# Attention of a hybrid encoder block: another deal of rows, tiles, banks and output turns

## The reference, cut to what matters

```python
h = rmsnorm(x, g_pre)
c_q, c_kv, k_pe, gate_a, hq, hf, hi, gate_b, merge_logits = split(h @ w_in)
...                                   # q, k (96 wide) and v (64 wide) for 8 heads
def one_block(args):                  # 128 queries of 2048, for each head
    sc = einsum('bhqd,bhkd->bhqk', qi, k) * scale
    sc = where(key_chunk <= query_chunk, sc, -inf)    # chunks of 64 frames
    p = softmax(sc)
    return einsum('bhqk,bhkd->bhqd', p, v)
y_a = (attn * silu(gate_a)) @ w_branch_a
...                                   # a second branch, a gated recurrence: y_b
y = (gate_0 * y_a + gate_1 * y_b) @ w_out
x = x + rmsnorm(y, g_post)
```

## Time and profile before

| | us |
|---|---|
| median of 3 runs | 2501.58 |
| lowest and highest | 2498.33, 2503.56 |
| profiled execution, its own time | 2496.99 |
| its span, first to last instruction | 2495.2 |

### The profile page before, as it was taken

One profiled execution on the slowest core, in us unless ns is written; L12 is line 12 of the kernel. 1 busy time (PEld: TensorE's weight loads), 2 busy tenths in 40 slices (PEclk: granted clock), 3 DMA queues, 4 the chain that ended last, 5 costly groups with the idle time before them and its releaser, 6 DMA issues. The chain is left out here.

```text
span 2495.2 us, 33539 instructions
## 1 busy us (share of the span) xinstructions
PE 2236.1 (90%) x11536; PEld 1853.5 (74%) x11536; DVE 1077.6 (43%) x1842; ACT 916.3 (37%) x1715; POOL 406.5 (16%) x254
## 2 busy tenths in 40 slices
PE   6999999999979999999678849988898875899998
PEld 5888888777868888888557737777777764677787
DVE  6000000000034554454356427767677766565663
ACT  7111111011034444444353216655655654343441
POOL 1222223214011111111022200000000003420220
PEclk9999999999989999999789859999999997899999
DMA  5222221223023333332665460223232107663751
GB/s 178 76 77 71 68 70 60 97 97 109 34 73 98 96 99 97 97 93 67 206 200 173 139 153 7 68 65 67 65 66 42 33 18 227 179 198 114 193 168 68
DMA packets 212448, 256.32 MB, mean 103 GB/s; under 512 B 38944, under 2 KB 137888, under 8 KB 208672
## 3 DMA queue, kind: packets, MB, share of 16 engines
q1 hardware_dynamic: 187616, 208.31, 29.4%
q10 hardware_dynamic: 23616, 43.00, 4.6%
q0 software_dynamic: 1152, 4.19, 0.5%
HBM read 157.41 MB, written 98.04 MB: 102 GB/s over the span
## 5 line engine op out<-in xcount | busy, mean ns | idle before, releaser
L1728 ACT ACTIVATE pT<-turn 128x512 fp32r<-128x512 f32 (+1 forms) x320 | 158.4, 533 | 203.5 <-PE turn L1855 202.9
L1785 DVE TENSOR_TENSOR pT<-turn,pT 128x512 fp32r<-128x512 f32 (+1 forms) x320 | 184.1, 606 | 92.5 <-ACT pT L1728 92.4
L66 PE MATMUL bankD<-hT_hi,shared_w_hi 128*128 128x512 f32 x512 | 212.2, 415 | 11.7 <-POOLq L676 11.7
L66 PE MATMUL bankA<-hT_hi,shared_w_hi 128*128 128x512 f32 x544 | 212.7, 391 | 0.0
L67 PE MATMUL bankA<-hT_lo,shared_w_hi 128*128 128x512 f32 x544 | 212.0, 390 | 0.0
L68 PE MATMUL bankA<-hT_hi,shared_w_lo 128*128 128x512 f32 x544 | 211.9, 390 | 0.0
L1771 DVE TENSOR_REDUCE chunk_min<-scores 128x1 f32<-128x512 f32 (+2 forms) x320 | 184.5, 606 | 61.3 <-PE scores L1841 37.3
L68 PE MATMUL bankD<-hT_hi,shared_w_lo 128*128 128x512 f32 x512 | 201.7, 394 | 0.0
L67 PE MATMUL bankD<-hT_lo,shared_w_hi 128*128 128x512 f32 x512 | 200.9, 392 | 0.0
L66 PE MATMUL scores<-k_sb,q_sb 96*128 96x512 f32 (+2 forms) x320 | 132.4, 414 | 73.3 <-ACT probs L1718 36.3
L1718 ACT ACTIVATE probs<-scores,least 128x1024 f32<-128x1024 f32 (+2 forms) x192 | 167.1, 871 | 38.5 <-DVE least L1778 37.4
(11 more groups left out here) (233 smaller groups left out, 4659.3 us busy)
## 6 DMA issues: line engine op xcount, KB each, us to landing
projT<-stage ACTq DMA_DIRECT2D x68, 256.0 KB, 2.4
shared_w_raw<-in_w_in_dram SPq DMA_DIRECT2D x32, 512.0 KB, 4.4
projT<-d_stage ACTq DMA_DIRECT2D x64, 256.0 KB, 2.4
e_l_in<-projT SPq DMA_DIRECT2D x64, 256.0 KB, 4.6
gateTok<-stage ACTq DMA_DIRECT2D x32, 256.0 KB, 2.0
shared_w_lo<-hgTok SPq DMA_DIRECT2D x16, 512.0 KB, 3.4
knT<-b_out SPq DMA_DIRECT2D x32, 256.0 KB, 2.8
vTok<-b_out SPq DMA_DIRECT2D x32, 256.0 KB, 2.9
```

Of the source, the lines that this page charges most:

```text
L66: pe.matmul(out, a_hi, b_hi, start=first, stop=False)
L1728: act.activation(pT[:, at % RING, 0, r0 * P:], turn[:, TURN_AT[tile] % 3, r0 * P:], ACT.Copy)\
L1785: dve.tensor_tensor(pT[:, at % RING, 1, r0 * P:], turn[:, TURN_AT[tile] % 3, r0 * P:], pT[:, at % RING, 0, r0 * P:].bitcast(F32), ALU.subt ...
```

## The change

The pieces of the diff stand in the order of the code: the schedule and the banks, the load of `fold`, then ACT's, DVE's and PE's parts.

```diff
-LED = 2 * TPB
+TURN_RING = 3
+LED = 2 * TPB + 1
...
+    TILES_AT = {9: 4, 10: 3, 11: 3, 12: 4, 13: 3, 14: 3, 15: 4,
+                0: 0, 1: 0, 2: 1, 3: 2, 4: 2, 5: 2, 6: 2, 7: 3, 8: 4}
...
     def s_bank(i, c):
-        return c + (r if b == 0 else 2 * (r % 2) if b == 1 else 0)
+        return (c + (r if b == 0 else 2 * (r % 2) if b == 1 else 3 * r if b == 2 else 0)) % 4
+    def chunks_of(i, piece):
+        b = i // TPB
+        cut = min(1 if s_bank(i, 0) == 3 else 2, b + 1)
+        return (0, cut) if piece == 0 else (cut, b + 1)
...
+        fold = sb("fold", [P, VD])
...
+                for half in range(2):
+                    sp.dma_start(fold[half * VD:(half + 1) * VD, :], ident_d[0:VD, 0:VD]).then_inc(const_in, 16)
...
-                        for tile in tiles[:AHEAD]:
-                            hi_part(h, tile)
                         if done is not None:
...
                             act.activation(oT[:], o_acc[:], ACT.Copy).then_inc(o_copied, 1)
+                        for tile in tiles[:AHEAD]:
+                            hi_part(h, tile)
...
-                            act.activation(o_lo[:], turn[:, at % 3].rearrange("p (t n) -> p t n", n=P)[:, :, VD:], ACT.Copy)\
-                               .then_inc(o_lo_ready, 1)
...
-                    dve.tensor_tensor(o_sum[:], turn[:, at % 3].rearrange("p (t n) -> p t n", n=P)[:, :, 0:VD], o_lo[:],
-                                      ALU.add).then_inc(o_sum_ready, 1)
...
-                    dve.tensor_tensor(o_out[:, b % 2], o_sum[:], inv[:].unsqueeze(2).to_broadcast([P, TPB, VD]), ALU.mult)\
-                       .then_inc(o_ready, 1)
+                    dve.tensor_tensor(o_out[:, b % 2], turn[:, at % TURN_RING, 0:TPB * VD].rearrange("p (t n) -> p t n", n=VD),
+                                      inv[:].unsqueeze(2).to_broadcast([P, TPB, VD]), ALU.mult).then_inc(o_ready, 1)
...
+                        if not tiles:
+                            for tile in before:
+                                values(h, tile, u)
+                            before = []
 ...
-                        for tile in tiles:
+                        for tile in before:
+                            if tile[0] == done:
+                                values(h, tile, u)
+                        for tile in tiles[:TURN_RING]:
                             transposes(h, tile)
                         for tile in before:
-                            values(h, tile, u)
+                            if tile[0] != done:
+                                values(h, tile, u)
+                        for tile in tiles[TURN_RING:]:
+                            transposes(h, tile)
...
-                                last = pe.transpose(turn[:, at % 3, r * P:(r + 1) * P], oT[:, r * P:(r + 1) * P], ident[:])
+                                last = pe.matmul(turn[:, at % TURN_RING, r * VD:(r + 1) * VD], oT[:, r * P:(r + 1) * P], fold[:], start=r == 0,
+                                                 stop=r == TPB - 1, skip_group_check=True)
```

More of the change, by code:

```diff
@@ L1529 @@
 AHEAD = 2
-LED = 2 * TPB
+TURN_RING = 3
+LED = 2 * TPB + 1
 def attention_schedule():
[L1537 to L1544, removed]
+    TILES_AT = {9: 4, 10: 3, 11: 3, 12: 4, 13: 3, 14: 3, 15: 4,
+                0: 0, 1: 0, 2: 1, 3: 2, 4: 2, 5: 2, 6: 2, 7: 3, 8: 4}
+    tiles = [(b, j) for b in range(NB) for j in range(TPB * (b + 1))]
+    steps = []
+    for row in [*range(LED, TT), *range(LED)]:
+        steps.append([row, tiles[:TILES_AT[row]], None, None])
+        tiles = tiles[TILES_AT[row]:]
     steps += [[None, [], None, None], [None, [], None, None]]
@@ L1587, in pieces_before @@
             if t < i:
-                b = t // TPB
-                used = {s_bank(t, x) for x in range(2 * piece, min(2 * piece + 2, b + 1))}
+                used = {s_bank(t, x) for x in range(*chunks_of(t, piece))}
                 if s_bank(i, c) in used:
@@ L1708, in exponentials @@
                     b, r = i // TPB, i % TPB
-                    first, end = 2 * piece, min(2 * piece + 2, b + 1)
+                    first, end = chunks_of(i, piece)
                     n = min(end * BLK, (i + 1) * P) - first * BLK
-                    bank = s_bank(i, 0)
-                    src = scores[:].rearrange("p b n -> p (b n)")[:, (bank + first) * BLK:(bank + first) * BLK + n]
+                    bank = s_bank(i, first)
+                    src = scores[:].rearrange("p b n -> p (b n)")[:, bank * BLK:bank * BLK + n]
                     if piece == 0:
@@ L1727, in hi_part @@
                     act.wait_ge(pv_done, h * TILES + (at + 2))
-                    act.activation(pT[:, at % RING, 0, r0 * P:], turn[:, TURN_AT[tile] % 3, r0 * P:], ACT.Copy)\
+                    act.activation(pT[:, at % RING, 0, r0 * P:], turn[:, TURN_AT[tile] % TURN_RING, r0 * P:], ACT.Copy)\
                        .then_inc(hi_ready, 1)
@@ L1735, in head @@
                     for i, tiles, done, o_block in STEPS:
-                        for tile in tiles[:AHEAD]:
-                            hi_part(h, tile)
+                        row_of = h + 1 if i is not None and i < LED else h
                         if done is not None:
@@ L1742, in head @@
                             act.activation(oT[:], o_acc[:], ACT.Copy).then_inc(o_copied, 1)
+                        for tile in tiles[:AHEAD]:
+                            hi_part(h, tile)
                         if i is not None and (more or i >= LED):
[L1744 removed]
+                            exponentials(row_of, i, 0)
                         for tile in tiles[AHEAD:]:
                             hi_part(h, tile)
[L1747 to L1753, removed]
[L1754 to L1755 removed]
+                        if i is not None and i >= 2 * TPB and (more or i >= LED):
+                            exponentials(row_of, i, 1)
                 for i in range(LED):
                     exponentials(0, i, 0)
+                    if i >= 2 * TPB:
+                        exponentials(0, i, 1)
                 with act.Fori(0, HEADS - 1) as h:
@@ L1784, in lo_part, with inverse @@
                     dve.wait_ge(hi_ready, h * TILES + (at + 1))
-                    dve.tensor_tensor(pT[:, at % RING, 1, r0 * P:], turn[:, TURN_AT[tile] % 3, r0 * P:],
+                    dve.tensor_tensor(pT[:, at % RING, 1, r0 * P:], turn[:, TURN_AT[tile] % TURN_RING, r0 * P:],
                                       pT[:, at % RING, 0, r0 * P:].bitcast(F32), ALU.subtract).then_inc(turn_read, 1)
-                def outputs(h, b):
-                    at = TURN_AT["o", b]
+                def inverse(h, b):
                     n = h * NB + (b + 1)
@@ L1811, in head @@
                 def head(h, more):
-                    for i, tiles, _, o_block in STEPS:
+                    for i, tiles, done, o_block in STEPS:
                         if i is not None and (more or i >= LED):
@@ L1854, in transposes @@
                     for r in range(max(0, j - TPB * b), TPB):
-                        last = pe.transpose(turn[:, at % 3, r * P:(r + 1) * P], probs[b][:, r, j * P:(j + 1) * P], ident[:])
+                        last = pe.transpose(turn[:, at % TURN_RING, r * P:(r + 1) * P], probs[b][:, r, j * P:(j + 1) * P], ident[:])
                     last.then_inc(turned, 1)
```

17 lines of the change are left out of this document (9 added, 8 removed).

## The result

| | before | after |
|---|---|---|
| median, us | 2499.95 (4 runs) | 2481.68 (4 runs) |
| profiled execution, us | 2496.99 | 2480.62 |
| its span, us | 2495.2 | 2478.8 |

The ratio is 0.9926, 95% interval 0.9904 to 0.9947: faster, by 0.7%. One of the four executions of after took 3248.95 us at a mean granted clock of 0.649 and is left out of the ratio; the median of the other three is 2480.62. The forecast was 2482.

The account below looks back on a forecast made before the run. TensorE sets the pace, through its waits, work and clock. A gain of 4 us net of waits and work plus 15 from the clock, 19 us, takes 2496.99 to 2478, median 2482; range 2465 to 2499.

Parts of the forecast that it names:

- seven heads at full clock: Seven heads of the attention: each goes from 68.2 to 67.4 us, 0.8 less, 5.6 for seven.
- last head: The final head, with no successor's rows 0 to 8: TensorE stands through copy and lo part, 1.4 us worse.
- Rotating banks and row 8 ahead: Row 9's step: its chunks go to banks 3, 0, 1, left long ago; row 8 fills TensorE before the last tiles.
- the 1.62 and the 0.29: TensorE's waits per head for bank 0, at row 9 (1.62 us) and row 10 (0.29); both were to go.
- The new waits: Waits inside a head that the change creates: 4.85 us, with refilling about 5.7.
- The fourth tile: Tile (0, 3) at row 9 wants the bank of (0, 0): a new wait of 1.0 us.
- the second pieces: Last chunks of rows 10, 13 and 14 wait 0.5, 0.5 and 0.1 us for the second pieces of rows' work.
- The early copy: ScalarE's copy ahead of hi parts: row 11 waits about 1.2 us, row 14 1.0; old 0.78, 1.78 and 0.74 go.
- The output product: Block ends: four products take 0.89 us, 0.45 more per block, 1.8 a head; removing copy and add gains nothing.
- Four passes: Skill's FP32 rule, not taken: at a record's length per pass, four output products take 1.8 us, 32 blocks 42 more.
- The clock: TensorE's clock in the heads: a quarter of the 19.8 us lost stays; gain 15, bounds 0 to 19.8.
- rival A: Waits move and the clock falls as often, transposes not counting as busy: only 4 us gained, 2497.6; chance 0.15.

Follow-up runs that it names:

- padding alone: The kernel before with four extra matmuls of 128 columns ahead of each block's output turn and no output product: 2525.05 us, ratio 1.0099.

## Why the prediction was right, and where its steps were off

The time was forecast within 2 us, whichever median is taken, and that is in good part luck: two errors of 7 and 8 us cancel. For the profiled execution, in us, said and measured: seven heads at full clock -5.6 and -12.6; clock -15, clock and loop end -6.9; last head +1.4 and +0.8; first wait +0.2 and +2.8; the first rows and the chance ahead of them, which no step had, -2.4 and +1.9. Together -19 and -16.4.

**Rotating banks and row 8 ahead.** Right that the 1.62 and the 0.29 go, the one by row 8's place, the other by the banks. Both edits are needed: with either undone 1.1 to 1.9 us a head come back.

**The new waits were over-sized.** The fourth tile waits 0.87 (said 1.0) and row 11 0.74 (said 1.2); row 14 waits 0.58 (said 1.0), the second pieces 0.14 or nothing (0.5, 0.5 and 0.1), and (2, 10) 0.12 (0.35). I had added ScalarE's durations end to end, with 0.2 us between engines. In its timeline the copy, two hi parts and the piece start 0.49 and then 0.96 us after one another, each a little ahead of the other's end: from the copy's start to the piece's end it is 2.58 us, not 2.8. That is half of the 0.4 at row 14; the rest isn't accounted for. The head came to 66.4, not 67.4, and the seven heads gained 12.6 instead of 5.6.

**The early copy.** It frees `o_acc` for block 2 (0.96 without it) and shortens row 11's wait, as costed; its price is the 0.58 at row 14.

**The output product.** 0.88 us for eight records, from 1924.46 to the next matmul at 1925.34, as taken from the earlier trace rows. Four passes, each as long as a record, would have been 1.8; that reading is not borne out, and how many passes a record holds the trace doesn't show. The step that failed is the one that costed the removed copy and add at nothing: in the new order they are worth 3.1 us a head (1.8 of work saved and still 1.3 lost), because VectorE stands for `o_lo` ahead of the minima and lo parts that come next in its list. That no wait of the earlier trace rows names them didn't make them free: with the product alone in the old order, row 15's wait of 0.74 shrank to 0.11, with padding alone to 0.36.

**The clock.** Right that falls behind row 9 and row 13 end. Wrong that a quarter of the loss stays: 23.8 us at 0.50 are left of 47.6, half. Of these, 10.2 stand at the loop end that stood still, and 13.6 behind a head's end, where I had called the waits too short. The trace of before already had such a fall, which the prediction overlooked when it said that no wait of 0.8 or less was followed by one. Its longest stretch at 0.50 begins behind the waits of 0.72 and 0.67 at a head's end, ahead of row 9's:

```profile
1774.06 0.49 PE L66 MATMUL scores<-k_sb,q_sb 96*128 96x512 f32 x1 [0.67 <-PE turn L1896]
...
1775.40:1785.60 10.20, 8.87 (x35) 7.79 (x34) 5.66 (x13) 3.95 (x10) 0.00 (x0) 0.50 0.93 186
```

Nor do such waits force a fall: with the old outputs in the new order they are there too (0.31 and 0.69), and five of seven heads keep 1.00. What decides is open. The loss itself was 21.6, not 19.8, as the earlier trace rows lack the first of the seven heads, which takes 70.1. The rule on transposes (rival A) would have left the falls behind row 11 and row 14, next to twelve transposes; there are none. But the waits there are 0.74 and 0.58, not the 1.0 to 1.2 that the rival counted on, so this doesn't refute the rule.

**The start and the last head.** With `fold` the first row waits about 2.5 us longer, not 0.2; its issue alone doesn't explain that, and what does is open. The last head lost 0.8 of the 1.4.

**What no step had** is the loop end, worth 6 us when it happens: the head with it takes 72.7, the other heads of that trace 66.4 to 69.4.

## What to carry to other kernels

When the clock of TensorE falls behind a wait, price that wait with the fall: filling 0.77 us of it with useless matmuls gave 8 us here by the medians, and placing a row's scores there 11 to 14, some of it perhaps luck at the loop ends. Weigh an intermediate by what stands behind it in each engine's list, not by whether the engine is busy on average. And count the instructions that an edit adds to a long loop body: 32 matmuls more cost a stop of 4 to 6 us at some loop ends.

## What the runs showed of the hardware

- TensorE's loop over two heads stands 3.8 to 5.8 us at some loop ends with 768 or 774 matmul records in its body, in eight of ten traces, with 9 more packets in the instruction queue for each. All 11 stops are at the ends of the first two passes of three, 20 places in these traces. With 736 or 746 records, in four traces, it never stood more than 0.71 at a loop end. The limit between them was not sought, nor why two traces with 768 are free of it.
- With TensorE kept at work at row 9 the granted clock was 1.00 in three of the seven heads instead of one, also with a DMA share of 0.28. Without it, it was 0.50 for 3.4 us or more behind waits of 1.70 and 1.78, and once for 10.2 us behind waits of 0.72 and 0.67.
- A plain float32 product of a 128x128 square with 64 columns takes two records of 0.11 us each, the same as with 128 columns: half the width saved nothing.
